# Output projections that fill the two memory attentions, as three fp32r products of split operands

## The reference

```python
def even_layer(x, mem, ...):
    h = rms_norm_2(x, norm_g) @ w_in
    y = jnp.concatenate([gdn_branch(...), diff_attention(...), memory_attention(...)], axis=-1)
    return x + y @ w_out          # w_out: 2560 x 2048

def memory_attention(q, gate, mem, mem_gain, w_kv, q_gain, k_gain):
    mk, mv = split_cols(rms_norm_2(mem, mem_gain) @ w_kv, [MEM_HEADS * MEM_DH, MEM_HEADS * MEM_DH])
    mk, q = rms_norm_2(mk by head, k_gain), rms_norm_2(q by head, q_gain)      # 4 heads of 128
    s = jnp.einsum('bqhd,bmhd->bhqm', q, mk).astype(F32) * (MEM_DH ** -0.5)
    p = jax.nn.softmax(s, axis=-1)
    return jnp.einsum('bhqm,bmhd->bqhd', p.astype(mv.dtype), mv) * jax.nn.silu(gate)
```

## Time and profile before

| | us |
|---|---|
| median of 3 runs | 2786.94 (2785.83 to 2787.17) |
| span of the profiled execution | 2787.4 |
| even layer, from the first DVE instruction of its memory attention (1992.96) to the first ACT instruction of the product behind it (2070.22) | 77.3 |
| odd layer, the same (2637.09 to 2714.45) | 77.4 |
| PE busy / DVE busy / ACT busy, whole span | 93% / 49% / 35% |

### The profile page before, as it was taken

The page is one execution under the profiler, slowest core; times in us unless marked ns, Lnnn a source line. Parts: engine busy times, 40 slices in busy tenths (PEclk is TensorE's granted clock), DMA queues, the critical chain, the costliest instruction groups (busy, mean ns, idle before and its releaser), DMA issues. The chain is left out here.

```text
span 2787.4 us, 38289 instructions
## 1 busy us (share of the span) xinstructions
PE 2598.2 (93%) x14362; PEld 1770.8 (64%) x14362; DVE 1354.9 (49%) x2599; ACT 976.6 (35%) x1730; POOL 105.2 (4%) x117
## 2 busy tenths in 40 slices
PE   8999999999888889999998999989899989988999
PEld 7984555887544444448975766855467746845757
DVE  5654784665311112226764545554535445464535
ACT  5544122444122122225524424432235414423424
POOL 0001111020011100010000000000000000001000
PEclk9999999999999999999999999999999989999999
DMA  7754433554499999984431114543334523431432
GB/s 302 216 211 156 138 138 141 186 199 147 160 422 422 422 421 422 399 344 161 169 122 67 38 57 166 189 173 106 106 136 141 200 85 141 154 122 75 148 109 91
DMA packets 80312, 529.66 MB, mean 190 GB/s; under 512 B 9089, under 2 KB 13569, under 8 KB 18849
## 3 DMA queue, kind: packets, MB, share of 16 engines
q1 hardware_dynamic: 76128, 514.50, 48.9%
q0 software_dynamic: 3456, 11.02, 1.6%
q10 hardware_dynamic: 576, 2.10, 0.2%
HBM read 520.24 MB, written 7.34 MB: 189 GB/s over the span
## 5 line engine op out<-in xcount | busy, mean ns | idle before, releaser
L379 DVE TENSOR_TENSOR split_wl<-ring,split_wh 128x512 fp32r<-128x512 f32 x480 | 331.0, 698 | 227.5 <-ACT split_wh L353 225.7
L353 ACT ACTIVATE split_wh<-ring 128x512 fp32r<-128x512 f32 x480 | 301.0, 631 | 291.6 <-PE ps L329 291.6
L327 PE MATMUL ps<-split_wh,split_xh 128*128 128x512 f32 x960 | 375.5, 391 | 0.0
L329 PE MATMUL ps<-split_wh,split_xl 128*128 128x512 f32 x960 | 373.6, 389 | 0.0
L328 PE MATMUL ps<-split_wl,split_xh 128*128 128x512 f32 x960 | 373.5, 389 | 0.0
L2132 PE MATMUL ps<-ring,yT 128*64 128x256 f32 x2048 | 247.8, 387 | 52.4 <-DMA ring<-in_weights 48.3
L631 PE MATMUL ps<-ring,xT 128*128 128x512 f32 x512 | 241.8, 625 | 29.9 <-issue 7.2
L434 PE MATMUL ps<-features_xh,features_wh 128*128 128x256 f32 x832 | 236.7, 285 | 1.5 <-DVE features_wl L425 1.5
L2132 PEld LDWEIGHTS ps<-ring,yT 128*64 128x64 f32 x2048 | 137.7, 137 | 155.4 <-DMA ring<-in_weights 91.0
L436 PE MATMUL ps<-features_xh,features_wl 128*128 128x256 f32 x832 | 235.3, 283 | 0.0
L631 PE MATMUL ps<-ring,yT 128*128 128x512 f32 x448 | 206.3, 612 | 20.9 <-issue 11.1
(11 more groups left out here) (630 smaller groups left out, 3389.9 us busy)
## 6 DMA issues: line engine op xcount, KB each, us to landing
ring<-in_weights SPq DMA_DIRECT2D x468, 1024.0 KB, 5.1
x_res<-in_x SPq DMA_DIRECT2D x1, 2048.0 KB, 7.5
yT<-in_mem SPq DMA_DIRECT2D x1, 2048.0 KB, 15.7
rel_skew<-lru_feat POOLq DMA_DIRECT2D x1, 2048.0 KB, 50.7
mem_features<-yT ACTq DMA_DIRECT2D x4, 512.0 KB, 6.6
s_wb<-in_s_bc POOLq DMA_DIRECT2D x4, 512.0 KB, 4.0
s_wc<-in_s_bc POOLq DMA_DIRECT2D x4, 512.0 KB, 3.9
gate_bias<-in_gate_bias POOLq DMA_DIRECT2D x8, 256.0 KB, 3.9
```

The costliest lines, as they stand in the source:

```text
L327: nc.tensor.matmul(out, xh[:, kc, at], wh[:, c % deep, :], start=kc == 0, stop=False)
L329: last = nc.tensor.matmul(out, xl[:, kc, at], wh[:, c % deep, :], start=False, stop=kc == chunks - 1)
L353: nc.scalar.activation(wh[:, c % deep, :], raw(unit, turn, c), ACT.Copy).then_inc(w_high.sem, 1)
L379: last = nc.vector.tensor_tensor(wl[:, c % deep, :], raw(unit, turn, c), wh[:, c % deep, :], ALU.subtract)
```

## The change

`memory_attention` makes its own fill, `SplitFill`, a subclass of `Fill`. Both memory attentions use it; the other users of `Fill` keep the plain one. In `SplitFill` each step is six fp32r products (three for each tile of 128 tokens) of split operands; ACT makes `wh` and `xh`, DVE `wl` and `xl`. There are 6 buffers of `wh` and `wl` (`DEEP`). Splits are made up to six steps ahead of the steps that the engine's place in the program has reached: `head_norm` begins with a call that makes the first six on ACT and DVE (`begin_act`, `begin_dve`), and each `store_act`/`store_dve` ends with making them up to six past its own count. `xl` lies in a part of `xT` that is free at that time. A slot of the ring is given back after the second product of its fourth chunk.

```diff
+class SplitFill(Fill):
+    DEEP = 6
...
+    def make_high(self, act, upto):
+        for step in range(self.high_at, min(upto, self.first[-1])):
+            if step in self.starts:
+                nc.scalar.activation(self.xh[:, part, :], self.x[:, part, :], ACT.Copy).then_inc(x_high.sem, 1)
+            slot = unit_wait(k, act, self.base + step // UNIT_KC, 0, 0)
+            act.wait_ge(w_used.sem, w_used.at(step - self.DEEP))
+            nc.scalar.activation(self.wh[:, step % self.DEEP, :], self.raw(slot, step), ACT.Copy).then_inc(w_high.sem, 1)
...
+    def make_low(self, dve, upto):
+        for step in range(self.low_at, min(upto, self.first[-1])):
+            if step in self.starts:
+                dve.wait_ge(x_high.sem, x_high.at(n))
+                nc.vector.tensor_tensor(self.xl[:, part, :], self.x[:, part, :], self.xh[:, part, :], ALU.subtract).then_inc(x_low.sem, 1)
+            dve.wait_ge(w_high.sem, w_high.at(step))
+            nc.vector.tensor_tensor(self.wl[:, step % self.DEEP, :], self.raw(slot, step), self.wh[:, step % self.DEEP, :], ALU.subtract)\
+                .then_inc(w_low.sem, 1)
...
+    def begin_dve(self, dve):
+        self.make_low(dve, self.DEEP)
...
+    def multiply(self, pe, steps):
...
+            if kc == 0:
+                pe.wait_ge(fill_a.sem, fill_a.at(n - 1))
+                pe.wait_ge(fill_v.sem, fill_v.at(n - 1))
+            pe.wait_ge(w_low.sem, w_low.at(step))
+            for t in range(NT):
+                nc.tensor.matmul(out, self.xh[:, kc, at], wh, start=kc == 0, stop=False)
+                mid = nc.tensor.matmul(out, self.xh[:, kc, at], wl, start=False, stop=False)
+                last = nc.tensor.matmul(out, self.xl[:, kc, at], wh, start=False, stop=kc == self.chunks - 1)
+            if step % UNIT_KC == UNIT_KC - 1:
+                mid.then_inc(k.unit_used, 1)
+            last.then_inc(w_used.sem, 1)
...
+    def store_dve(self, dve, steps):
+        self.dve_at += steps
+        while self.dve_done < len(self.blocks) and self.first[self.dve_done + 1] <= self.dve_at:
+            self.make_low(dve, self.first[n + 1])
+            dve.wait_ge(w_used.sem, w_used.at(self.first[n + 1] - 1))
+            dve.wait_ge(fill_a.sem, fill_a.at(n))
+            self.blocks[n][3][1](dve, n, 3).then_inc(fill_v.sem, 1)
+            self.dve_done += 1
+        self.make_low(dve, self.dve_at + self.DEEP)
...
 # head_norm
             @block.vector
             def _(dve):
+                if fill:
+                    fill.begin_dve(dve)
...
             @block.scalar
             def _(act):
+                if fill:
+                    fill.begin_act(act)
                 act.wait_ge(ms.sem, ms.at(0))
```

More of the change, by code:

```diff
@@ L635, in multiply, with begin_act @@
             self.pe_at = step + 1
+    def begin_act(self, act):
+        pass
+    def begin_dve(self, dve):
+        pass
     def store_act(self, act, steps):
@@ L660, in end, with __init__, raw, begin_act @@
         self.k.ended(fill_a=len(self.blocks), fill_v=len(self.blocks))
+class SplitFill(Fill):
+    DEEP = 6
+    def __init__(self, k, scope, x, chunks, blocks, out, low):
+        super().__init__(k, (x, chunks, blocks, out))
+        self.x, self.chunks = x, chunks
+        self.xh = k.sb(scope, "fill_xh", [P, chunks, SEQ], F32R)
+        self.xl = low
+        self.wh, self.wl = (k.sb(scope, f"fill_w{n}", [P, self.DEEP, BLK], F32R) for n in "hl")
+        self.pieces = first_pieces(chunks)
+        self.starts = [p.start for p in self.pieces]
+        self.high_at = self.low_at = 0
+    def raw(self, slot, step):
+        c = step % UNIT_KC
+        return self.k.ring[:, slot, c * BLK:(c + 1) * BLK]
+    def make_high(self, act, upto):
+        k, nc = self.k, self.k.nc
+        x_high, w_high, w_used = k.ev("x_high"), k.ev("w_high"), k.ev("w_used")
+        for step in range(self.high_at, min(upto, self.first[-1])):
+            if step in self.starts:
+                part = self.pieces[self.starts.index(step)]
+                nc.scalar.activation(self.xh[:, part, :], self.x[:, part, :], ACT.Copy).then_inc(x_high.sem, 1)
+            slot = unit_wait(k, act, self.base + step // UNIT_KC, 0, 0)
+            act.wait_ge(w_used.sem, w_used.at(step - self.DEEP))
+            nc.scalar.activation(self.wh[:, step % self.DEEP, :], self.raw(slot, step), ACT.Copy).then_inc(w_high.sem, 1)
+            self.high_at = step + 1
+    def make_low(self, dve, upto):
+        k, nc = self.k, self.k.nc
+        x_high, x_low, w_high, w_low = k.ev("x_high"), k.ev("x_low"), k.ev("w_high"), k.ev("w_low")
+        for step in range(self.low_at, min(upto, self.first[-1])):
+            if step in self.starts:
+                n = self.starts.index(step)
+                part = self.pieces[n]
+                dve.wait_ge(x_high.sem, x_high.at(n))
+                nc.vector.tensor_tensor(self.xl[:, part, :], self.x[:, part, :], self.xh[:, part, :], ALU.subtract).then_inc(x_low.sem, 1)
+            slot = (self.base + step // UNIT_KC) % RING
+            dve.wait_ge(w_high.sem, w_high.at(step))
+            nc.vector.tensor_tensor(self.wl[:, step % self.DEEP, :], self.raw(slot, step), self.wh[:, step % self.DEEP, :], ALU.subtract)\
+                .then_inc(w_low.sem, 1)
+            self.low_at = step + 1
+    def begin_act(self, act):
+        self.make_high(act, self.DEEP)
+    def begin_dve(self, dve):
+        self.make_low(dve, self.DEEP)
+    def multiply(self, pe, steps):
+        k, nc = self.k, self.k.nc
+        fill_a, fill_v, x_low, w_low, w_used = (k.ev(n) for n in ("fill_a", "fill_v", "x_low", "w_low", "w_used"))
+        for step in range(self.pe_at, min(self.pe_at + steps, self.first[-1])):
+            n, kc = divmod(step, self.chunks)
+            if kc == 0:
+                pe.wait_ge(fill_a.sem, fill_a.at(n - 1))
+                pe.wait_ge(fill_v.sem, fill_v.at(n - 1))
+            if step in self.starts:
+                pe.wait_ge(x_low.sem, x_low.at(self.starts.index(step)))
+            pe.wait_ge(w_low.sem, w_low.at(step))
+            wh, wl = self.wh[:, step % self.DEEP, :], self.wl[:, step % self.DEEP, :]
+            for t in range(NT):
+                out, at = k.ps[:, 6 + t, :], slice(t * P, (t + 1) * P)
+                nc.tensor.matmul(out, self.xh[:, kc, at], wh, start=kc == 0, stop=False)
[4 more added lines that the diff above has]
+            last.then_inc(w_used.sem, 1)
+            self.pe_at = step + 1
+    def store_act(self, act, steps):
+        k, fill_a, w_used = self.k, self.k.ev("fill_a"), self.k.ev("w_used")
+        self.act_at += steps
+        while self.act_done < len(self.blocks) and self.first[self.act_done + 1] <= self.act_at:
+            n = self.act_done
+            self.make_high(act, self.first[n + 1])
+            act.wait_ge(w_used.sem, w_used.at(self.first[n + 1] - 1))
+            self.blocks[n][3][0](act, n, 3).then_inc(fill_a.sem, 1)
+            self.act_done += 1
+        self.make_high(act, self.act_at + self.DEEP)
+    def store_dve(self, dve, steps):
+        k, fill_a, fill_v, w_used = self.k, self.k.ev("fill_a"), self.k.ev("fill_v"), self.k.ev("w_used")
+        self.dve_at += steps
+        while self.dve_done < len(self.blocks) and self.first[self.dve_done + 1] <= self.dve_at:
+            n = self.dve_done
+            self.make_low(dve, self.first[n + 1])
[4 more added lines that the diff above has]
+        self.make_low(dve, self.dve_at + self.DEEP)
+    def end(self):
+        assert self.high_at == self.first[-1] and self.low_at == self.first[-1]
+        steps, pieces = self.first[-1], len(self.pieces)
+        super().end()
+        self.k.ended(x_high=pieces, x_low=pieces, w_high=steps, w_low=steps, w_used=steps)
@@ L2924, in memory_keys, with memory_attention @@
     return kv
-def memory_attention(k, tag, qg, kv, gain_q, gain_k, fill):
+def memory_attention(k, tag, qg, kv, gain_q, gain_k, before, out):
     n = MEM_HEADS * P
[L2930 to L2940, removed]
+    with ExitStack() as parts:
+        low = k.nc.alloc_sbuf_tensor_at(f"{tag}_fill_xl", [P, HEADS, SEQ], F32R, offset=k.xT_at + 4 * 4 * SEQ)
+        fill = SplitFill(k, parts, before, HEADS, D // BLK, out, low)
+        with ExitStack() as inner:
+            scratch = k.sb(inner, f"{tag}_sq", [P, n])
+            head_norm(k, [v[:, t, 0:n].rearrange("p (h w) -> p h w", w=P) for v in (qg, kv) for t in range(NT)], P, scratch,
+                      fill=fill, steps=6)
+        attention(k, MEM_HEADS, times_row(k, lambda h: qg[:, :, ds(h * P, P)], k.row(gain_q)),
+                  times_row(k, lambda h: kv[:, :, ds(h * P, P)], k.row(gain_k)),
+                  lambda h, kt: kv[:, kt, ds(h * P + n, P)], lambda h: qg[:, :, ds(h * P, P)], float(P) ** -0.5,
+                  fill=fill, steps=(3, 3, 2, 2))
+        times_silu(k, [qg[:, t, 0:n] for t in range(NT)], [qg[:, t, n:2 * n] for t in range(NT)], fill, 6,
```

(2 more changed lines are left out.)

7 lines of the change are left out of this document (3 added, 4 removed).

## The result

The changed kernel takes 2803.84 us (median of 4 runs, 2803.58 to 2805.34) against 2787.06 for the kernel before, measured with it: ratio 1.0057, 95% interval 1.0045 to 1.0068. It is 16 to 17 us slower; 12 were forecast. The profiled execution has a span of 2801.9 us, 14.5 more than the one of before.

A forecast was written before the change was run, and what follows sets the result against it. PE bounds the stretch as a whole, but DVE has only some 1.3 us of room in the head norm. Terms sum to +5.8 us a layer, +11.6 for two, giving 2799 us; range 2789 to 2806.

The forecast's parts named there:

- the prediction's own signs of being wrong: Head norm still about 11 us, a fill step slower than 1.36 us, or staging to layer end not under 66.4 us.
- staging later, head norm bound by DVE: Head norm: DVE's added splits around the norm put the first staging at 20.5 us instead of 10.98, +9.5 us a layer.
- first score later, cold restart: Behind the first staging: PE's idle 11 us halves the clock for the first pair's transposes and scores, +0.9 us.
- bank add to step 9: Attention: from DVE's first bank add to PE's step 9 takes 6.2 us instead of 4.5, +1.7 us.
- steps 9 to 31: Rest of the fill: PE is last again and 23 steps save 0.36 us each, -8.3 us a layer.
- end of the attention: Last splits wait for buffers of steps 24 and 25, so the engines meet later, +1.6 us.
- silu: In `times_silu`, PE reaches its transposes after 2.7 us but the silu product ends at 3.2 us, +0.4 us.
- Step 14 ahead of staging: Before the second pair's staging, DVE's split for this step waits for step 8's buffer; part of a +1.7 us term.
- the clock costs more: Rival, chance 0.14: low clock also covers steps 9 to 11, another 1.6 us a layer, giving +7.4 a layer, 2802.
- The Trainium skill's count of passes: PE's fill steps: FP32 takes four passes, so three would save 0.43 us a step, not 0.36; not used.
- The rivals of the other side: Gain case, chance 0.06: splits fall into DVE's idle time and PE's whole saving stands, -11.5 us a layer, 2764.
- A covered gain (2764): Same gain case, chance 0.06: DVE's 50 us of idle time in the stretch absorbs the splits, -11.5 us a layer.

The follow-up runs named there:

- first-six-only kernel: Changed kernel making only the six splits ahead of the head norm in each layer, later steps reusing those buffers (does not compute the reference): 2784.8 us, ratio 0.9985.
- four-ahead kernel: Changed kernel with each store call making splits up to 4 steps past its own count instead of 6, still 6 buffers: 2797.6 us, ratio 1.0031.
- busy-PE kernel: Changed kernel with 21 dummy f32 products on PE behind its six steps of the head norm: 2799.6 us, ratio 1.0038.
- odd-only kernel: Changed kernel with split operands only in the odd layer's memory attention, the even layer keeping the plain fill: 2797.4 us, ratio 1.0036.

## Why the prediction was right, and where it was off

The direction, the mechanism and the range (2789 to 2806) held; the forecast was 2799 for 2803.84. Two of the prediction's own signs of being wrong came up all the same: a fill step takes 1.39 us, not 1.36, and the time from staging to the end of the layer, 66.4 before and forecast at 62.7, is 64.2 in the odd layer but 66.5 in the even one, where nothing was gained behind the head norm. What failed there is sizes (the pace and the clock, below), not the order of the engines. Step by step, odd layer, with the even one in brackets where it differs; each against the corresponding time of before:

| term | predicted | measured |
|---|---|---|
| staging later, head norm bound by DVE | +9.5 | +9.08 (+9.08) |
| first score later, cold restart | +0.9 | +1.4 (+1.6) |
| bank add to step 9 | +1.7 | +1.9 (+2.3) |
| steps 9 to 31 | -8.3 | -7.4 (-5.6) |
| end of the attention | +1.6 | +1.5 |
| silu | +0.4 | +0.4 |
| sum | +5.8 | +6.9 (+9.3) |

- *What bounds the stretch.* Right. Mean shares (DVE 27.55 of 77.40) would have said that there is room for the splits; the timeline of the head norm said 1.3 us. The first-six-only kernel shows that this piece alone is worth the whole gain of PE.
- *Staging.* The series in front was priced by the same series at the start of another product; its last split ends at 6.8 us instead of 7.04 (the third piece of `xl` starts 0.2 us sooner behind ACT's high part; no run tells why), and the meeting of the engines at the block's end at 0.32 us instead of 0.45.
- *The clock at the restart* was mis-sized: 0.9 taken, 1.4 to 1.6 measured. It was a slip in adding up: four transposes at 0.11 and four scores at 0.23 make 1.36 us, which a halved clock doubles, and that is what came. In the odd layer the first transpose to the first score product takes 1.83 us for 1.37, and from there to DVE's first score 2.11 for 1.17. With 1.36 the forecast for a layer would have been +6.3. The busy-PE kernel removes just this term.
- *Step 14 ahead of staging.* Right in kind and size, shown by the four-ahead kernel, where it goes.
- *Steps 9 to 31.* The term that failed most. The pace of 1.36 us a step was read from a product loop; in the fill, a step takes 1.39 (the third product of one step is at 2683.24, that of the next at 2684.64: 1.40), so 0.33 is saved, not 0.36. Over 23 steps that is 0.7 of the 0.9 us missing in the odd layer; the rest isn't traced. In the even layer there are 1.8 us more: the clock was at its low level over the nine products from step 9 to the middle of step 10, at 0.43 us each instead of 0.23. That is the rival "the clock costs more", which I had at 0.14 and 2802; the measured case is my forecast in one layer and that rival in the other, and which layer gets which is luck (the odd-only kernel had it the other way in its odd layer).
- *The Trainium skill's count of passes* ("FP8 and Floating Point Precision", section "TensorE Precision Notes") would have made a step 1.29 us. The measured pace is 1.39, farther off than the pace in the loop: the rows were the better guide, and even they were too fast.
- *The rivals of the other side.* A covered gain (2764) did not come, for the reason given. Part of it can be had: 2770.8, with the splits where there is room, of which the split operands are 11.4 us and the banks the rest.

## What to carry to other kernels

An engine that is busy 35% of a stretch may still have no room in the piece of it that counts: before work is given to it, look in the timeline, block by block, for what it has in front of the next meeting of the engines, and put the added instructions behind what others wait for, not ahead of it. Work made ahead should stay far enough behind the newest step of its consumer that no wait in it stands in front of urgent work: four ahead with six buffers was better than six by 6 us in the medians and by 5.7 in the two stretches. And an idle stretch of PE has a second price, the products behind it at half pace: 21 dummy products in a gap of 10 us saved 1.3 to 1.4 us of it a layer, but not the slow products behind the shorter gaps that follow.

## What the runs showed of the hardware that was not expected

- The same three fp32r products have a pace of 0.227 us each in the product loop and 0.232 in the fill, at the same granted clock of 1.00 (2604 to 2610 us of before, 2682.7 to 2687.0 us of the changed kernel). No run here tells why.
- The same code, two layers, differs by 2 us with where the stretch of low clock falls: in the changed kernel step 9 and half of step 10 ran at 0.50 in the even layer and at 1.00 in the odd one, in the odd-only kernel at 0.50 in the odd one. Idle stretches of 3.0 to 3.1 and of 2.2 us stood ahead in all three.
- In the kernel of before with two pairs of banks, where PE's longest idle stretch is 1.61 us, both layers take 73.88 us, at a granted clock of 1.00 where it had been 0.98. So part of the gain from the banks is clock.
